# FFN up-projection with the tokens as stationary operand, block transposes on VectorE, and a new order of the tail

## The reference, cut to what matters

```python
def causal_dwconv(u, w, b):                 # CONV_WIDTH = 3
    S = u.shape[1]
    up = jnp.pad(u, ((0, 0), (CONV_WIDTH - 1, 0), (0, 0)))
    y = b
    for j in range(CONV_WIDTH):
        y = y + w[j] * up[:, j:j + S]
    return y
...
        h2 = rmsnorm(x, ffn_norm_w[l])
        up = causal_dwconv(h2 @ w_ffn_up[l], conv_w[l], conv_b[l])   # 2048 x 11264
        a, b = jnp.split(up, 2, axis=-1)
        x = x + (jax.nn.silu(a) * b) @ w_ffn_down[l]                 # 5632 x 2048
```

## Time and profile before

| what | value |
|---|---|
| median of three runs | 2452.24 us |
| the profiled execution, its own time | 2452.33 us |
| its span | 2450.5 us |
| TensorE matmul busy | 2443.6 us (100%) |
| TensorE weight load busy | 2043.6 us (83%) |
| VectorE busy | 1525.5 us (62%) |
| ScalarE busy | 1233.7 us (50%) |
| granted TensorE clock | 1.0 in all of the span |
| FFN stage, first up matmul to start of `mem1` | 734.2 to 1445.3 us |

### The profile page before, as it was taken

The page is one execution under the profiler, slowest core; times in us unless marked ns, Lnnn a source line. Parts: engine busy times, 40 slices in busy tenths (PEclk is TensorE's granted clock), DMA queues, the critical chain, the costliest instruction groups (busy, mean ns, idle before and its releaser), DMA issues.

```text
span 2450.5 us, 35584 instructions
## 1 busy us (share of the span) xinstructions
PE 2443.6 (100%) x11789; PEld 2043.6 (83%) x11789; DVE 1525.5 (62%) x1808; ACT 1233.7 (50%) x1628; POOL 228.8 (9%) x250
## 2 busy tenths in 40 slices
PE   9999999999999999999999999999999999999999
PEld 7888888878888888888888888888887888888887
DVE  5445545587877777777777776454456645555564
ACT  6445454555455444444444445454556555655443
POOL 0021223231000000000000000010001100520000
PEclk9999999999999999999999999999999999999999
DMA  7554555566655555555555556854454545544655
GB/s 268 196 182 171 173 176 177 188 228 226 206 195 175 190 195 187 191 188 188 189 190 190 189 190 212 251 183 170 171 184 160 181 163 179 178 164 157 226 185 163
DMA packets 134819, 464.17 MB, mean 189 GB/s; under 512 B 14544, under 2 KB 21328, under 8 KB 134112
## 3 DMA queue, kind: packets, MB, share of 16 engines
q1 hardware_dynamic: 122464, 443.08, 53.6%
q10 hardware_dynamic: 12256, 20.15, 2.5%
q0 software_dynamic: 32, 0.03, 0.0%
HBM read 455.87 MB, written 7.34 MB: 189 GB/s over the span
## 4 chain that ended last, share of the span: by engine, by line
PE 98%; DVE 1%; issue 1%; ACT 0%; DMA 0%; POOL 0%; ACTq 0%; POOLq 0%; DVEq 0%
PE PS L641 21%; PE PS L643 21%; PE PS L642 21%; PE PS L890 13%; PE PS L895 7%; PE PS L917 3%; PE PS L918 3%; PE PS L919 3%; PE PS L752 1%; PE PS L723 1%; PE PS L682 1%; PE PS L703 1%; PE PS L731 0%; DVE WL L1603 0%; DMA RAW<-w_stream 0%
## 5 line engine op out<-in xcount | busy, mean ns | idle before, releaser
L1603 DVE TENSOR_TENSOR WL<-RAW,WH 128x1024 fp32r<-128x1024 f32 x842 | 1058.6, 1260 | 871.2 <-ACT WH L1099 865.2
L1099 ACT ACTIVATE WH<-RAW 128x1024 fp32r<-128x1024 f32 x841 | 889.7, 1060 | 1110.4 <-PE PS L643 725.2
L641 PE MATMUL PS<-WH,HT 128*128 128x512 f32 (+1 forms) x1816 | 720.1, 397 | 0.2 <-DVE WL L1603 0.2
L643 PE MATMUL PS<-WH,HT 128*128 128x512 f32 (+1 forms) x1816 | 706.9, 389 | 0.0
L642 PE MATMUL PS<-WL,HT 128*128 128x512 f32 (+1 forms) x1816 | 705.6, 389 | 0.0
L641 PEld LDWEIGHTS PS<-WH,HT 128*128 128x128 f32 x1816 | 341.2, 188 | 72.0 <-issue 5.3
L643 PEld LDWEIGHTS PS<-WH,HT 128*128 128x128 f32 x1816 | 340.8, 188 | 71.6
L642 PEld LDWEIGHTS PS<-WL,HT 128*128 128x128 f32 x1816 | 341.4, 188 | 66.6
L890 PE MATMUL PS<-HT,WH 128*128 128x512 f32 x1408 | 352.8, 392 | 0.0
L890 PEld LDWEIGHTS PS<-HT,WH 128*128 128x128 f32 x1408 | 253.7, 189 | 45.7
L895 PEld LDWEIGHTS PS<-HT,WL 128*128 128x128 f32 x1408 | 192.2, 190 | 13.8
(11 more groups left out here) (301 smaller groups left out, 1907.8 us busy)
## 6 DMA issues: line engine op xcount, KB each, us to landing
RAW<-w_stream SPq DMA_DIRECT2D x841, 512.0 KB, 3.3
bias_scratch<-BE ACTq DMA_DIRECT2D x12, 256.0 KB, 4.0
MEMR<-mem_in ACTq DMA_DIRECT2D x1, 2048.0 KB, 11.6
X<-x_in ACTq DMA_DIRECT2D x4, 512.0 KB, 4.4
x_scratch<-X ACTq DMA_DIRECT2D x4, 512.0 KB, 4.6
X<-x_scratch ACTq DMA_DIRECT2D x1, 2048.0 KB, 9.0
out<-X ACTq DMA_DIRECT2D x8, 256.0 KB, 3.1
X<-x_in SPq DMA_DIRECT2D x3, 512.0 KB, 9.2
```

Of the source, the lines that this page charges most:

```text
L641: pe.matmul(o, hi, WH[:, slot, kk, 0:cols], start=k == 0, stop=False)
L643: ins = pe.matmul(o, lo, WH[:, slot, kk, 0:cols], start=False, stop=k == nq * GK - 1)
L1099: act.activation(WH[:, g.slot(j)], RAW[:, g.slot(j)], ACT.Copy).then_inc(hi_split, 1)
L1603: dve.tensor_tensor(WL[:, s], RAW[:, s], WH[:, s].bitcast(F32), ALU.subtract).then_inc(lo_split, 1)
```

## The change

TensorE: `ffn_up` now takes HT[:, k, hi or lo, 128 tokens] as stationary and the weights as moving operand, as `rows_product` does. The result has tokens on the partitions and needs no second half, so a unit takes two banks: banks 2 and 3 for unit a, 0 and 1 for unit b. The chunks of the down projection take banks 4, 6, 2, 4 (in the last one 4, 0, 6, 4).

VectorE: `up_turn` transposes the unit from PSUM to FU in square blocks of 32x32, 16 instructions of 32 partitions and 2x4x32 elements each, in four parts of four instructions. `down_add` adds one chunk at a time, at steps 18, 20, 22, 23. `conv` has two taps left; the product comes two tiles to a step; `block_lo` is in two halves.

ScalarE: no copies from PSUM any more; `taps` computes the first tap with its bias (Identity with a scale and a bias from PARAM), `block_hi` is in two halves.

`ffn_free`, `ffn_copied` and `ffn_sum` are replaced by `up_turned` (one for each unit), `down_added` (one for each chunk, four given at the start) and `ffn_tap`. FY has four tiles, FC is gone.

```diff
-                                for kk in range(GK):
-                                    k = q * GK + kk
-                                    pe.matmul(PS[:, half + f, :], WH[:, slot, kk, f * P:(f + 1) * P], HT[:, k, :, :],
-                                              start=k == 0, stop=False, skip_group_check=True)
...
+                        for kk in range(GK):
+                            k = q * GK + kk
+                            for t in range(T):
+                                hi, lo = HT[:, k, 0, t * P:(t + 1) * P], HT[:, k, 1, t * P:(t + 1) * P]
+                                o = PS[:, bank + t, :]
+                                pe.matmul(o, hi, WH[:, slot, kk, :], start=k == 0, stop=False)
+                                pe.matmul(o, hi, WL[:, slot, kk, :], start=False, stop=False)
+                                ins = pe.matmul(o, lo, WH[:, slot, kk, :], start=False, stop=k == KT - 1)
...
             with pe.Fori(0, FB - 1) as b:
                 g = At(g0 + 2 * GD, b, 3 * GD)
+                pe.wait_ge(up_turned, At(1, b, 2).count())
+                pe.wait_ge(down_added, At(3, b, 4).count())
+                ffn_up(g, At(2, b, 2), 0)
+                pe.wait_ge(up_turned, At(2, b, 2).count())
+                ffn_up(g, At(3, b, 2), GD)
...
+                ffn_down(g, 2 * GD, At(0, b, 2), (4, 6, 2, 4), chunk_free)
+            pe.wait_ge(up_turned, 2 * FB - 1)
+            pe.wait_ge(down_added, 4 * FB - 1)
             straight("mem1", 1, GD, MEMT)
...
+            def up_turn(u, end, parts):
+
+                dve.wait_ge(group_used, end)
+                bank = 0 if u.base % 2 else 2
+                for a in parts:
+                    for c in range(4):
+                        src = PS[32 * a:32 * a + 32, bank:bank + 2, :].rearrange("p t (f d) -> p t f d", f=FT)[:, :, :, 32 * c:32 * c + 32]
+                        dst = FU[32 * c:32 * c + 32, :, 2:S + 2].rearrange("p f (t s) -> p t f s", t=T)[:, :, :, 32 * a:32 * a + 32]
+                        ins = dve.transpose(dst, src)
+                if 3 in parts:
+                    ins.then_inc(up_turned, 1)
...
+            def down_add(c, bank, end):
...
+                dve.tensor_tensor(o, PS[:, bank:bank + 2, :], o, ALU.add).then_inc(down_added, 1)
...
+                    if p < 4:
+                        up_turn(At(1, b, 2), g.count(), (p,))
+                    if p in (6, 7):
+                        for f in (2 * p - 12, 2 * p - 11):
+                            gated(f, At(FT, b, 2 * FT), b * FT + NFT // 2, At(FT, b, FT).count())
+                    if 8 <= p < 12:
+                        up_turn(At(2, b, 2), g.count(GD), (p - 8,))
+                    if p == 12:
+                        block_lo(At(0, b, 2), 0)
+                        block_lo(At(0, b, 2), 1)
...
+                    if p in (18, 20, 22, 23):
+                        c = (18, 20, 22, 23).index(p)
+                        down_add(c, (4, 6, 2, 4)[c], g.count(2 * GD + 2 * c + 2))
...
+                if p < 2:
+                    up_turn(At(2 * FB - 1), GROUP0["mem1"], (2 * p, 2 * p + 1))
+                if p in (3, 4):
+                    for f in (2 * p - 6, 2 * p - 5):
+                        gated(f, At(2 * FT * FB - FT), NFT - FT, FB * FT)
+                if p in (5, 6):
+                    block_lo(At(2 * FB - 2), p - 5)
```

More of the change, by code:

```diff
@@ L897, in body, with ffn_down @@
                         return ins
                     group(g, j + q, body)
-            def ffn_down(g, u, j, blk, products_before=None):
+            def ffn_down(g, j, blk, banks, free):
                 for c in range(NCH):
[L903 to L909, removed]
+                    free(c)
@@ L910, in ffn_down @@
                     for q in range(2):
+                        if c == 0:
+                            pe.wait_ge(ffn_lo, blk.count(q + 1))
                         def body(slot):
@@ L1379, in _ @@
                 split(At(g0), p + RING)
[L1380 to L1386, removed]
+                if p == 13:
+                    taps(At(0), 0, None)
+                if p == 15:
+                    silu(At(0), 0)
+                    silu(At(0), 1)
+            silu(At(0), 2)
+            silu(At(0), 3)
             with act.Fori(0, FB - 1) as b:
@@ L1390, in _ @@
                     split(g, p + RING)
[L1391 to L1397, removed]
+                    if p == 5:
+                        taps(At(1, b, 2), b * FT + NFT // 2, None)
+                    if p == 9:
+                        act.wait_ge(group_used, g.count())
+                        block_hi(At(0, b, 2), 0)
+                        block_hi(At(0, b, 2), 1)
+                    if p == 13:
+                        taps(At(2, b, 2), b * FT + FT, At(2, b, 2).count())
+                    if p in (15, 16):
+                        for f in (2 * p - 30, 2 * p - 29):
+                            silu(At(2 * FT, b, 2 * FT), f)
             for p in range(GD):
@@ L1909, in down_add, with gated @@
-            def down_add(u, end):
-                dve.wait_ge(group_used, end)
-                half, c0 = 4 * (u.base % 2), 2 * (u.base % 2)
-                for c in range(2):
-                    o = X[:, :, (c0 + c) * CH:(c0 + c + 1) * CH]
-                    ins = dve.tensor_tensor(o, PS[:, half + 2 * c:half + 2 * c + 2, :], o, ALU.add)
-                ins.then_inc(ffn_free, 1)
+            def gated(f, tile, feature, silu_done):
+                conv(f, tile, feature)
+                dve.wait_ge(ffn_conv, tile.count(f + 1))
+                dve.wait_ge(ffn_silu, silu_done)
+                ins = dve.tensor_tensor(FP[:, f, :], FA[:, f, :], FY[:, f, :], ALU.mult)
+                if f % 2:
+                    ins.then_inc(ffn_prod, 1)
```

146 lines of the change are left out of this document (66 added, 80 removed).

## The result

The changed kernel takes 2460.11 us (median of 8 runs, 2459.19 to 2460.88) against 2452.29 us before (8 runs, 2452.16 to 2452.41): ratio 1.0032, interval 1.0024 to 1.0041. It is slower by 7.8 us. The stated range (2447 to 2465) holds this. The single number (2455) is 5.1 us low, the measured time is 1.1 us above what the forecast's own case allowed (2451 to 2459), and "the same within 0.2%" was called likeliest where "slower by over 0.2%" came out. The profiled execution took 2459.5 us with a span of 2457.7, 7.2 over the span before.

A forecast was written before the change was run, and what follows sets the result against it. TensorE was taken to bound the kernel, with 98% of the chain of waits. Up groups -12.9, head waits +11.0 and tail +4.5 summed to +2.6 us on the profiled 2452.33, giving 2455 us, range 2447 to 2465.

The forecast's parts named there:

- the forecast's own case: All terms as forecast, or with transposes overlapping: 2451 to 2459 us (head waits 9.5 to 14, tail 2.5 to 5.9), chance 0.57.
- The up groups, -12.9 us: TensorE's up units: 176 groups take 2.72 us in place of 2.793, each 0.073 us shorter.
- The head waits, +11.0: Pass heads: TensorE waits for VectorE's third add, queued behind step 22's split; 1.1 us at ten places, 9.5 to 14 together.
- the row of the weight load: Profile row on TensorE restarting after a VectorE result: one-hot instruction ended at 512.64, weight load began at 512.70.
- Rival 1: Head wait met in time, the third add coming before group 23 ends: 2443.8 us, chance 0.10.
- The transposes, 0.465: VectorE's `up_turn`: instructions changing partitions don't overlap, so each costs 0.465 us, between 0.352 and 0.55.
- Rival 4: VectorE's transposes overlap after all, 0.352 us each: 2452.8 us; chance counted within the forecast's own case.
- No loss inside a pass: VectorE finishes the first half of `block_lo` before TensorE's group 16, with 0.6 us in hand; cost nothing.
- Rival 2: VectorE late in every pass, TensorE waiting before group 16, from 0.50 us a transpose: 2464.2 us, chance 0.30.
- Pass 0, costed like the others: First loop pass: no term of its own for VectorE or ScalarE lateness; its head wait excused by four given counts.
- The tail, +4.5: Behind the loop: TensorE waits once for `block_lo` before the last down projection, 4.5 us, between 2.5 and 5.9.
- The call "same": Whole kernel: time within 0.2% of before, 2447.3 to 2457.1 us, chance 0.52, against 0.37 slower and 0.11 faster.

The follow-up runs named there:

- one: Changed kernel with VectorE adding the third chunk of a down projection at step 21 of a pass, not step 22: 2448.21 us, 0.9983 of the kernel before.
- seven: Changed kernel with third add at step 21, reordered taps and block_lo behind the loop, first unit's taps, convolution and silu a step earlier: 2441.02 us, 0.9954.
- four: Changed kernel with each transpose writing the partitions it reads, so the output order differs from the reference's: 2456.48 us, 1.0018 of the kernel before.
- experiment three: Changed kernel with 16 unused matmuls into an idle PSUM bank before the wait of the last down projection: 2458.08 us, 1.0024 of the kernel before.
- six: Changed kernel with the first unit's taps, convolution and silu one step earlier, before the loop: 2458.78 us, 1.0027 of the kernel before.
- eight: Changed kernel with the first tap and its bias back on VectorE and no taps on ScalarE: 2483.25 us, 1.0126 of the kernel before.

## Why the prediction was right or wrong, point by point

- **The up groups, -12.9 us: right.** Groups start 2.72 us apart, and with the new waits gone (one and seven) each pass is 1.17 us shorter than before.
- **The head waits, +11.0: right,** in place, cause and size. 1.17 each, 11.7 by the trace and 11.9 by taking them away, inside the bounds of 9.5 to 14. The 0.1 for the empty pipe stood on no row of the prediction and was found at each head (0.33 in place of 0.227); the release took 0.14 where the row of the weight load gave 0.06. Rival 1 fell. Experiment one makes it true, at 2448.2 where its price was 2443.8; most of the 4.4 between them are pass 0, the tail and the clock, below.
- **The transposes, 0.465: right,** 0.455, and for the reason given (four). Its three parts add up to 0.463, and no row was named for the last, 0.035. Rival 4, that they overlap after all, fell with it.
- **No loss inside a pass: right for passes 1 to 9,** with about 0.3 us in hand where 0.6 was forecast. Rival 2 didn't come in the form given, but its point was well placed: with a fifth transpose it came, and its price there (2.6 us a pass) was undervalued by the expectation, since the model had no path from late transposes over ScalarE's taps to late splits.
- **Pass 0, costed like the others: wrong, 1.5 us.** So small a slack is as good as the state in which the loop is entered. The entry was not followed on VectorE and ScalarE.
- **The tail, +4.5: the mechanism right, the term too small.** The gap cost 4.84 and its restart 0.1. Of the 0.4 more, most is ScalarE's taps, sized at 1.5 us from the earlier trace rows and in fact 2.08 for four, with the WH of step 3 behind them:

```profile
1459.71 2.08 ACT L1374 ACTIVATE FY<-FU,PARAM 128x256 f32<-128x256 f32 x4 [4.36 <-DVE FU L1904]
```

- **The clock behind the gap: not foreseen, 1.6 us by the trace and 2.0 by the medians of experiment three.** The gap itself was forecast, and what a gap of that length does to the matmuls behind it was not asked. This is the largest piece missing from the sum.
- **The call "same": wrong.** The sum was +2.6, and the line of "slower" lay at +4.9. What it lacked (heads 0.7, pass 0 1.5, tail 0.4, clock 1.6) was small each time and had the same sign each time.
- **The range: met in part by luck.** 2460.11 lies outside the forecast's own 2451 to 2459. The stated range reached that far for the sake of rival 2, which did not come; what filled the room was pass 0 and the clock, which the prediction had no term for.

## What to carry to other kernels

Moving the last consumer of a buffer behind an instruction that waits for the newest data makes TensorE wait for the whole chain; look for the step before it. When an engine's slack is under half a microsecond, follow it from the entry of the loop to its exit, over every engine that stands behind it: the steady pass came out as forecast, with 0.3 us of slack less, and both ends did not. A gap of some microseconds on TensorE should be priced with the matmuls behind it as well.

## What the runs showed that was not expected

- After 5.07 us between two starts (the changed kernel, one and six) TensorE's matmuls began at the lower clock at once; after 4.94 us (eight) and 3.60 us (four) the clock fell with the third matmul. After 1.3 us (ten heads) or with 16 matmuls in the gap it didn't happen.
- The stretch at 0.43 per matmul had no fixed length: behind the same gap it was 3.45 us in the profile of the changed kernel, 4.4 in that of six and 5.2 in that of one.
- A matmul that restarts TensorE at the full clock mostly shows 0.49 to 0.50 us and its successor starts 0.31 to 0.34 later, not 0.227: about 0.1 us for each stop, of 0.5 us (pass 0) or of 5 (eight).
- ScalarE's copy of 256 columns with a scale and a bias from PARAM takes 0.52 us in a row of four, against 0.39 with a scale alone and 0.295 without. That the bias makes the difference is inferred from these rows and wasn't tested by itself.
